# Product-key scatter: one 256-column matmul for each token, low halves added by VectorE, low splits of the stage made by GpSimd

## What is computed

```python
v_half, i_half = lax.top_k(s, PEER_TOPK)
...
experts = (i1 * PEER_KEYS + i2).reshape(T, PEER_HEADS * PEER_TOPK)
gates = jax.nn.softmax(best, axis=-1).reshape(T, PEER_HEADS * PEER_TOPK)
...
u = expert_u[eb]
act = jax.nn.gelu(jnp.einsum('td,tkd->tk', xb, u), approximate=False) * gb
return jnp.einsum('tk,tkd->td', act, expert_v[eb])
```

## Time and profile before

| | us |
|---|---|
| median of 3 runs (1753.81 to 1756.58) | 1756.58 |
| the profiled execution, time | 1751.53 |
| its span in the profile | 1749.9 |
| TensorE busy | 1689.0 (97%) |
| VectorE busy | 1303.8 (75%) |
| ScalarE busy | 1023.4 (58%) |
| GpSimd busy | 119.4 (7%) |

### The profile page before, as it was taken

How to read it: one execution, slowest core, us unless ns; L and a number is a source line. 1 busy time by engine, 2 the same in 40 slices (tenths; PEclk the granted TensorE clock), 3 DMA queues, 4 the chain that set the end, 5 groups by cost and what they waited for, 6 DMA issues and landing times.

```text
span 1749.9 us, 34534 instructions
## 1 busy us (share of the span) xinstructions
PE 1689.0 (97%) x10926; PEld 1521.9 (87%) x10926; DVE 1303.8 (75%) x2377; ACT 1023.4 (58%) x1567; POOL 119.4 (7%) x105
## 2 busy tenths in 40 slices
PE   7999999999999999999999999999999998899997
PEld 7998889999999999988888888898878887778886
DVE  6866665599977777777777777789777777877776
ACT  7653445666656666655545555664476666666665
POOL 0022300234320000000000000000000000000000
PEclk9999999999999999999999999999999999999999
DMA  6542246476775555567777777553356554246553
GB/s 203 166 147 73 85 157 208 154 226 202 221 233 176 178 170 177 176 209 242 240 267 245 242 241 241 178 169 106 109 160 198 183 190 151 85 137 210 182 192 108
DMA packets 114411, 316.65 MB, mean 181 GB/s; under 512 B 12752, under 2 KB 45904, under 8 KB 113840
## 3 DMA queue, kind: packets, MB, share of 16 engines
q1 hardware_dynamic: 113504, 311.88, 55.4%
q0 software_dynamic: 848, 4.00, 0.7%
HBM read 296.95 MB, written 18.87 MB: 180 GB/s over the span
## 4 chain that ended last, share of the span: by engine, by line
PE 83%; DVE 10%; ACT 3%; issue 2%; DMA 1%; POOL 1%; ACTq 0%; DVEq 0%; SPq 0%
PE bank L324 10%; PE bank L325 10%; PE bank L326 10%; PE bank L259 9%; PE bank L260 9%; PE bank L280 9%; PE bank L261 9%; PE bank L284 5%; PE bank L1327 3%; DVE wlo L243 2%; PE bank L1769 1%; PE bank L1034 1%; ACT whi L235 1%; POOL wlo L1626 1%; DVE arena L1493 1%
## 5 line engine op out<-in xcount | busy, mean ns | idle before, releaser
L243 DVE TENSOR_TENSOR wlo<-raw,whi 128x1024 fp32r<-128x1024 f32 x495 | 608.0, 1230 | 148.7 <-ACT whi L235 138.1
L235 ACT ACTIVATE whi<-raw 128x1024 fp32r<-128x1024 f32 x524 | 550.1, 1052 | 45.0 <-PE bank L318 34.4
L259 PE MATMUL bank<-x,whi 128*128 128x256 f32 (+1 forms) x1728 | 508.6, 294 | 8.9 <-DVE wlo L243 4.0
L261 PE MATMUL bank<-x,wlo 128*128 128x256 f32 (+1 forms) x1728 | 492.0, 285 | 0.0
L260 PE MATMUL bank<-x,whi 128*128 128x256 f32 (+1 forms) x1728 | 491.7, 285 | 0.0
L259 PEld LDWEIGHTS bank<-x,whi 128*128 128x128 f32 x1728 | 331.8, 192 | 15.2 <-issue 13.1
L260 PEld LDWEIGHTS bank<-x,whi 128*128 128x128 f32 x1728 | 332.5, 192 | 0.1
L261 PEld LDWEIGHTS bank<-x,wlo 128*128 128x128 f32 x1728 | 331.6, 192 | 0.0
L324 PE MATMUL bank<-whi,yhi 128*128 128x512 f32 x816 | 320.1, 392 | 8.9 <-DVE ylo L1596 3.1
L325 PE MATMUL bank<-wlo,yhi 128*128 128x512 f32 x816 | 318.6, 390 | 0.0
L326 PE MATMUL bank<-whi,ylo 128*128 128x512 f32 x816 | 318.1, 390 | 0.0
(11 more groups left out here) (313 smaller groups left out, 1753.9 us busy)
## 6 DMA issues: line engine op xcount, KB each, us to landing
raw<-in_stream SPq DMA_DIRECT2D x524, 512.0 KB, 3.5
act_spill<-h SPq DMA_DIRECT2D x128, 128.0 KB, 3.2
h<-act_spill SPq DMA_DIRECT2D x128, 128.0 KB, 3.3
h<-in_x SPq DMA_DIRECT2D x1, 1024.0 KB, 5.3
arena<-in_keys POOLq DMA_DIRECT2D x1, 1024.0 KB, 6.3
h_spill<-h SPq DMA_DIRECT2D x1, 1024.0 KB, 8.0
arena<-h_spill POOLq DMA_DIRECT2D x1, 1024.0 KB, 7.3
arena<-in_g_final POOLq DMA_DIRECT2D x1, 512.0 KB, 9.2
```

Source lines behind the costliest of these rows:

```text
L235: nc.scalar.activation(whi[:, q * 1024:(q + 1) * 1024], raw[:, q * 1024:(q + 1) * 1024], ACT.Copy).then_inc(hi_ready, 1)
L243: nc.vector.tensor_tensor(wlo[:, q * 1024:(q + 1) * 1024], raw[:, q * 1024:(q + 1) * 1024], whi[:, q * 1024:(q + 1) * 1024].bitcast(F32), ...
L259: nc.tensor.matmul(bank[b][:, 0:T], whi[:, w], xhi[:, x], start=k == 0, stop=False)
L261: last = nc.tensor.matmul(bank[b][:, 0:T], wlo[:, w], xhi[:, x], start=False, stop=k == KT - 1)
```

## The change

For each token the one-hot of i1 (now HOT1) goes without the gate. The gate goes with i2: HOT2 is a tile of 128 x 256, with the gate's high part at column i2 of its left half and the low part at column i2 of its right half. One fp32r matmul of 256 columns gives both halves of the token's part of G side by side in PSUM. ScalarE copies the high halves of four tokens to G (`g_high`), and VectorE adds the low halves to it in place (`sums`, with one input and the output in G, at the step of 256 words). The PSUM banks are declared as one tensor, and a slab's four tokens take two banks. `I1T` and `GT_COLS` now stay in PSUM; the gate's two parts (`GATES`), `I2T` and `iota` are in SBUF.

VectorE has four instructions for single tokens (`one_token`, a scalar_tensor_tensor over 256 elements), two for pairs of tokens (`two_tokens`, a tensor_tensor over 256) and a sum for each slab. It makes no low splits in this stage: GpSimd makes all 64 (`low_split`). TensorE takes a token behind every second chunk (k = 1, 3, 5, 7), and a slab's `slabs_done` comes ahead of its last token. Buffers: HOT1 holds four tokens, HOT2 two.

```diff
+        banks = ctx.enter_context(nc.psum_tensor("bank", [P, 8 * 512], F32))
+        bank = [banks[:, i * 512:(i + 1) * 512] for i in range(8)]
...
-                if between and k == KT // 2 - 1:
-                    between()
-            last.then_inc(slabs_done, 1)
+                if k == KT - 1:
+                    last.then_inc(slabs_done, 1)
+                if between:
+                    between(k)
...
+        GATES = h[:, 4 * SEQ:6 * SEQ].rearrange("p (s t) -> p s t", s=2)
+        I1T, I2T = bank[6][:, 0:SEQ], h[:, 6 * SEQ:7 * SEQ]
+        GT_COLS = bank[7][:, 0:SEQ]
...
+        HOT1 = (ylo[:, 0:SEQ], ylo[:, SEQ:2 * SEQ])
+        HOT2 = [yhi[:, b * SEQ:(b + 1) * SEQ].rearrange("p (s k) -> p s k", s=2) for b in range(2)]
+        SUMS = [banks[:, (2 + 2 * b) * 512:(4 + 2 * b) * 512].rearrange("p (t s k) -> p t s k", s=2, k=P)
+                for b in range(2)]
...
+            def token(i, r, y):
+
+                pe.wait_ge(s("hot_a"), i * (4 * TPS) + r * TPS + y + 1)
+                if y % 2 == 0:
+                    pe.wait_ge(s("hot_b"), i * 8 + r * 2 + y // 2 + 1)
+                if y == 0:
+                    pe.wait_ge(s("g_sum"), i * 4 + r + 1)
+                nc.tensor.matmul(SUMS[r % 2][:, y, :, :], HOT1[y // 2][:, y % 2 * P:(y % 2 + 1) * P], HOT2[y % 2],
+                                 start=True, stop=True).then_inc(s("hot_free"), 1)
...
-                up(pe, N_U + E1, U_U + E1, i, r, 4, SEQ, between=lambda: pair(i, r, 0))
-                pair(i, r, 1)
+                up(pe, N_U + E1, U_U + E1, i, r, 4, SEQ, between=lambda k: token(i, r, k // 2) if k % 2 else None)
...
-                nc.scalar.activation(dst, bank[2 + r % 2][:, 0:TPS * KEYS].rearrange("p (t k) -> p t k", k=KEYS),
-                                     ACT.Copy).then_inc(s("g_evac"), 1)
+                nc.scalar.activation(dst, SUMS[r % 2][:, :, 0, :], ACT.Copy).then_inc(s("g_high"), 1)
...
-                chain.link(nc.vector.tensor_copy(h[:, 4 * SEQ:6 * SEQ], bank[4][:, :]))
+                chain.link(nc.vector.tensor_copy(I2T, bank[6][:, SEQ:2 * SEQ]))
                 dve.wait_ge(s("gate_cols"), 1)
+                chain.link(nc.vector.tensor_tensor(GATES[:, 1, :], GT_COLS, GATES[:, 0, :], ALU.subtract))
...
+            def one_token(k0, i, r, y):
+                n = i * (4 * TPS) + (k0 + r) * TPS + y
                 dve.wait_ge(s("hot_free"), n - 2 + 1 + TPS)
+                own = slice(n, n + 1) if isinstance(n, int) else bass.ds(n, 1)
+                nc.vector.scalar_tensor_tensor(out=HOT2[y % 2], in0=iota[:, :].unsqueeze(1).to_broadcast([P, 2, P]),
+                                               scalar=I2T[:, own], in1=GATES[:, :, own].to_broadcast([P, 2, P]),
+                                               op0=ALU.is_equal, op1=ALU.mult).then_inc(s("hot_a"), 1)
+
+            def two_tokens(k0, i, r, z):
+                n = i * (4 * TPS) + (k0 + r) * TPS + 2 * z
+                dve.wait_ge(s("hot_free"), n - 4 + 2 + TPS)
+                c2 = I1T[:, n:n + 2] if isinstance(n, int) else I1T[:, bass.ds(n, 2)]
+                nc.vector.tensor_tensor(HOT1[z].rearrange("p (t k) -> p t k", k=P),
+                                        iota[:, :].unsqueeze(1).to_broadcast([P, 2, P]),
+                                        c2.unsqueeze(2).to_broadcast([P, 2, P]),
                                         ALU.is_equal).then_inc(s("hot_b"), 1)
 
+            def sums(k0, i, r):
...
+                dve.wait_ge(s("g_high"), k + 1)
...
+                nc.vector.tensor_tensor(dst, dst, SUMS[(k0 + r) % 2][:, :, 1, :], ALU.add).then_inc(s("g_sum"), 1)
+
+            def step(k0, i, r, first=False, last=False):
+                one_token(k0, i, r, 1)
+                two_tokens(k0, i, r, 1)
+                one_token(k0, i, r, 2)
+                one_token(k0, i, r, 3)
+                if not first:
+                    sums(k0 - 1, i, r)
+                if not last:
+                    two_tokens(k0 + 1, i, r, 0)
+                    one_token(k0 + 1, i, r, 0)
...
+            sums(KEYS - E1 - 1, 0, 0)
+            dve.wait_ge(lo_ready, N_V + AHEAD)
...
+            def low_split(i, r):
+                q = slot(N_U + E1 + AHEAD, r)
+                pool.wait_ge(lo_ready, at(N_U + E1 + AHEAD, i, r, 4))
+                pool.wait_ge(hi_ready, at(N_U + E1 + AHEAD, i, r, 4) + 1)
+                nc.gpsimd.tensor_tensor(wlo[:, q * 1024:(q + 1) * 1024], raw[:, q * 1024:(q + 1) * 1024],
+                                        whi[:, q * 1024:(q + 1) * 1024].bitcast(F32), ALU.subtract)\
+                    .then_inc(lo_ready, 1)
+
+            steps(pool, KEYS - E1, 4, low_split)
```

More of the change, by code:

```diff
@@ L151, in build @@
         arena = sb("arena", 32768)
-        bank = [ctx.enter_context(nc.psum_tensor(f"bank{i}", [P, 512], F32)) for i in range(8)]
+        banks = ctx.enter_context(nc.psum_tensor("bank", [P, 8 * 512], F32))
+        bank = [banks[:, i * 512:(i + 1) * 512] for i in range(8)]
         def V(name, i=0, n=1):
@@ L1310, in pe_peer @@
                                          GATE[:, tt * NHK:(tt + 1) * NHK])):
-                    last = nc.tensor.transpose(bank[4 + x // 2][:, (x % 2) * SEQ + tt * P:(x % 2) * SEQ + (tt + 1) * P],
+                    last = nc.tensor.transpose(bank[6 + x // 2][:, (x % 2) * SEQ + tt * P:(x % 2) * SEQ + (tt + 1) * P],
                                                src, ident[:, :])
@@ L1339, in act_peer @@
         def act_peer(act, chain):
-            act.sem_inc(s("g_evac"), 2)
+            act.sem_inc(s("g_sum"), 2)
             turn_act(act, T_WQ)
@@ L1378, in act_peer @@
             act.wait_ge(s("h_spilled"), 16)
-            nc.scalar.activation(GT_COLS, bank[5][:, 0:SEQ], ACT.Copy).then_inc(s("gate_cols"), 1)
+            nc.scalar.activation(GATES[:, 0, :].bitcast(F32R), GT_COLS, ACT.Copy).then_inc(s("gate_cols"), 1)
             for k in range(COLS_AT, E1):
@@ L1558, in four_tokens @@
[L1558 to L1563, removed]
-                                        ALU.is_equal).then_inc(s("hot_b"), 1)
@@ new lines, in sums @@
+            def sums(k0, i, r):
+                k = at(k0, i, r, 4)
+                dve.wait_ge(s("g_high"), k + 1)
+                g3 = G[:, :].rearrange("p (k t) -> p t k", t=SEQ)
+                dst = g3[:, k * TPS:k * TPS + TPS, :] if isinstance(k, int) else g3[:, bass.ds(k * TPS, TPS), :]
+                nc.vector.tensor_tensor(dst, dst, SUMS[(k0 + r) % 2][:, :, 1, :], ALU.add).then_inc(s("g_sum"), 1)
[9 more added lines that the diff above has]
+                    one_token(k0 + 1, i, r, 0)
@@ L1582, in prod @@
+            two_tokens(0, 0, 0, 0)
+            one_token(0, 0, 0, 0)
+            step(0, 0, 0, first=True)
+            steps(dve, KEYS - E1 - 2, 4, lambda i, r: step(1, i, r))
+            step(KEYS - E1 - 1, 0, 0, last=True)
+            sums(KEYS - E1 - 1, 0, 0)
+            dve.wait_ge(lo_ready, N_V + AHEAD)
             def prod(k0, i, r):
@@ L1598, in prod_lo @@
                     .then_inc(y_lo, 1)
-            dve.wait_ge(s("g_evac"), KEYS - E1 + 2)
+            dve.wait_ge(s("g_sum"), KEYS - E1 + 2)
             prod(0, 0, 0)
```

17 lines of the change are left out of this document (4 added, 13 removed).

## The result

The changed kernel takes 1865.57 us (median of 4 runs, 1863.56 to 1868.71), against 1756.57 for the kernel before: a ratio of 1.063, with a 95% interval of 1.0615 to 1.0643. That is 109 us more. The profiled execution took 1868.71 us, with a span of 1867.1. The two profiled executions lie 117 us apart, 8 more than the medians: the one of the kernel before took 1751.5, one of its shortest, and the one of the change was the longest of its four.

What follows compares the result with a forecast made beforehand. TensorE's own instructions were taken to bound the scatter stage; VectorE tokens held by GpSimd's splits would raise a slab from 3.76 to 5.30 us. 1751.5 + 98.6 (64 slabs) + 1.1 (last sum) = 1851 us, range 1785 to 1905.

Steps and rivals of the forecast that it cites:

- case one: Scatter slab: GpSimd's split holds token 2; its matmul and the last six chunk matmuls follow, 5.34 us a slab.
- the two heaps: Sign in the scatter's token instructions on VectorE: durations fall into two groups, 0.48 and about 2 us.
- the 0.28: Sign on VectorE in the scatter: held token instructions end 0.28 us after a GpSimd split.
- the 64 splits of 2.4: Sign on GpSimd in the scatter: 64 low splits of 2.4 to 2.8 us each.
- the loop: Scatter: slab's end, gelu, high split, GpSimd's split, held token, remaining matmuls, next slab's end; taken as 5.30 us a slab.
- the two cases: Scatter: token 2 held, 5.34 us each slab; or token 3, then next slab's token 0, 5.34 or 5.19 each.
- The preparation of the columns: Done once: a copy halved, a subtraction of 256 added; with the moved slab semaphore under 0.5 us, taken as nothing.
- (a): Rival, scatter: tokens are held but the phases fit, 4.28 us a slab, 1786 us in all; chance 0.09.
- (b): Rival, scatter: a sum of 1.55 us leaves VectorE never idle, 5.57 a slab, 1868, or 5.9 and 1890; chance 0.11.
- (c): Rival, scatter: TensorE's clock falls to 1.2 GHz after idling, 45 us on top of 1844: 1889 us; chance 0.15.
- (d): Rival, scatter: tokens aren't held; 1727 us at TensorE's 3.36 a slab, 1748 if a ring of 3.69 binds; chance 0.08.
- a ring: Scatter with free tokens: token 1's matmul, token 3, sum, one-hots, token 0, back to token 1's matmul: 3.69 us.

Runs made afterwards that it cites:

- the fastest version: The change with gates in PSUM, sum ahead of token 3, G's step only in the sum's write, and ScalarE's copy ahead of its high split: 1735.2 us.

## Why the prediction was right, and where not

**The mechanism and its price.** 1851 us was forecast and 1865.6 measured. The decisive step, that a token instruction with two SBUF inputs can't run beside GpSimd's split and ends 0.28 behind it, is shown twice: by the trace of the change (607.62 to 607.91) and by the gates in PSUM, which free the tokens and give back 86.6 us. There 127 token instructions run wholly inside a split of GpSimd, and none is held. Which token is held, the prediction left open; it is case one, token 2, in 63 of 64 slabs, at 5.33 of the 5.34 forecast.

**One reading was weaker than it was put.** That an operation with one input in PSUM isn't held was read from 0.27 "in the midst of GpSimd's". That row starts at 200.97, where GpSimd's ends at 201.13: the two overlap by 0.16 only, and the 0.27 is also the only price that was taken for such an instruction. The conclusion holds, by the 127 of the run with the gates in PSUM. Of the signs named, the two heaps, the 0.28 and the 64 splits of 2.4 came; TensorE idled for (240.00 - 173.45) / 44.1 = 1.5 us a slab (44.1 slabs of 5.44) where 1.9 was said, and the sum took 1.36 instead of 1.10.

**Terms of the loop.** Three were off and cancel, which is luck. The prediction had 0.12 + 0.72 = 0.84 from the held token's matmul to token 3's. It is 0.93, since the first matmul behind a wait takes 0.38 and the next starts 0.22 later. Against these 0.09, GpSimd starts 0.08 behind the high split instead of 0.15, and TensorE 0.12 behind VectorE instead of 0.14. The gelu's 0.20, the high split's 0.28 and 1.05, the split's 2.39 and the 0.28 behind it are as in the earlier trace rows.

**From 5.34 to 5.41.** Every fourth slab takes 5.66: the split's starts at 610.57 and 616.23, where 605.23 to 610.57 is 5.34. That is where the loop over four slabs turns, and ScalarE shows it:

```profile
614.60 0.38 ACT L1363 ACTIVATE h<-bank 128x256 f32<-128x256 f32 x1 [3.11 <-PE bank L262]
615.09 1.06 ACT L236 ACTIVATE whi<-raw 128x1024 fp32r<-128x1024 f32 x1
```

The gelu starts 0.30 behind token 3's matmul (614.30) instead of 0.20, and the high split 0.49 behind the gelu instead of 0.28. The slab behind it takes 5.42. It wasn't in the sum: the mean of the four is 5.44, and the first slab, 3.48 with nothing held yet, brings the stage's mean to 5.41. I had taken 5.30, between the two cases, so 0.11 a slab or 7 us in 64 were too little.

**The sum of the change.** Of the span's +117.2 (1867.1 - 1749.9), the stage is 344.9 - 239.1 = +105.8, where the prediction had +98.6. Behind the stage come +4.8 instead of +1.1. The last sum makes an idle stretch of TensorE of 4.14 us (2.63 in the earlier trace rows), +1.5; after it the matmuls start 0.43 apart and the stretch 873 to 886 has a clock of 0.74, where 757 to 770 had 1.00, another +2.6.

```profile
874.10 0.77 PE L326 MATMUL bank<-whi,yhi 128*128 128x512 f32 x1 [4.14 <-DVE ylo L1609]
874.67 0.63 PE L327 MATMUL bank<-wlo,yhi 128*128 128x512 f32 x1
875.09 0.63 PE L328 MATMUL bank<-whi,ylo 128*128 128x512 f32 x1
```

The prediction counted the sum's own time and not the clock behind it. The last 0.7 comes far behind, in code that both kernels share. The remaining +6.6 lies ahead of the scatter, in shared code too: in 120 to 140 us the clock was 0.83 instead of 1.00, and in 220 to 240 it was 0.74 instead of 0.92. Why, no run tells; it is most of the 8 us by which the profiled executions lie further apart than the medians. In the fastest version it was 0.91 and 0.83 there, and its stage begins 3.6 later than before's. The preparation of the columns costs nothing, as assumed: from TensorE's last wait ahead of it to the first scatter matmul are 28.2 us (496.57 to 524.8) against 28.8.

**The sum over G.** 1.10 was taken, 1.36 measured, inside the bounds of 0.685 and 1.55. In the change itself this makes no difference, since it lies in the shadow of the held token. It counts as soon as the tokens are free.

**The rivals.** (a), phases that fit at 4.28, didn't come: with two tiles of HOT2 nothing can be stored up. (b), a sum dear enough to keep VectorE busy, didn't either: its 1.36 lies below the 1.55. (c), the lower clock, came in the kernel without a step in G, where TensorE idles for 2.28; in the change its waits are 0.56 and 0.91 long, 1.24 where the loop turns, and the clock is 1.00. (d), tokens that aren't held, is the kernel with the gates in PSUM, at 1779 instead of 1748, for a ring that is 0.47 longer than forecast.

**What stands and what is open.** The cheaper matmul is real: TensorE alone has 3.36 a slab, and the last version comes within 0.07 of it. The low splits on GpSimd cost 44 to 47 us in the old kernel. In the new one the holding costs some 87 with the splits on GpSimd, and having them there instead of on VectorE, in this order of work, 17. With the gates in PSUM no wait for them shows. Taking the step out of the copy's write and the sum's read gave 29 us, and the order of copy and high split 19, once the tokens are free. Not settled is why the clock is at 0.95 in the change with the sum ahead of token 3, and at 1.00 in the change: TensorE's idle stretches are much alike (0.46 and 1.05, and at most 1.27, against 0.56, 0.91 and at most 1.24). Nor is it known whether the fastest version owes something to GpSimd at all: it wasn't tried with the splits on VectorE. The 3.3 us that VectorE has to do for each slab there, with 1.15 more for a split, are more than the 3.43 of a slab, which speaks against it, but that is argued and not shown.

## What to carry to other kernels

Before work goes from VectorE to GpSimd, list the operands of what stays on VectorE in those stretches. In these traces an instruction with one of its tensors in PSUM runs on. One with two tensors in SBUF, or a tensor_scalar from SBUF to SBUF, stands still for as long as a single GpSimd instruction lasts, and so does what is queued behind it. Operands in SBUF alone don't decide: in the kernel before, the search for the top 16, on one tensor in SBUF, goes on inside GpSimd's split of 365.48 to 367.89 in its usual time.

```profile
365.51 0.41 DVE L1441 MAX8 arena<-arena 128x8 f32<-128x256 f32 x1
```

A move of an operand, or shorter GpSimd instructions, can be worth more than the work that was moved. And when a held engine is freed, walk the ring through the smallest buffer at once, with each wait's order on every engine in it: here it took three more steps, of 4, -29 and -19 us, before the cheaper matmul was worth anything.

## What was not expected of the hardware

- A step of 256 words in G costs each side of VectorE's 512-element sum: 0.68 us with none, 1.09 where only the write has it, 1.36 where read and write have it. ScalarE's copy of 512 takes 0.59 dense and 1.10 with it. The Trainium skill ("VectorE: DVE Perf Modes", the section on the TRN2 errata) gives one formula for an fp32 tensor_tensor, an estimate of 0.69 for 512 elements; the dense run agrees, and the other two don't.
- What holds VectorE is a single instruction of GpSimd: with four GpSimd instructions of 0.85 in the mean instead of one of 2.39, a token's mean time fell from 920 ns to 538.
- A tensor_scalar over 128 elements with a single tensor input in SBUF and two column operands is held too, 1.88 for two instead of 0.60. How far behind GpSimd's end a held instruction ends goes with its form: 0.08 for this one, 0.28 for the token's 256 elements, and 0.41 for a tensor_tensor over 384 in the kernel before (163.92 + 1.21 = 165.13, beside a GpSimd instruction that ends at 164.72).
- TensorE's first matmul behind a wait takes 0.38 instead of 0.28, and the next one starts 0.22 behind it instead of 0.12.
- After 2.28 us idle (G without a step) and after 4.14 (the transition of the change) TensorE's clock was at the lower level; after 2.63 in the kernel before it stayed at the full one. The length of the pause alone doesn't decide.
- A loop written out for four slabs costs at its turn: 5.66 instead of 5.34 in the change, where ScalarE comes late, and some 3.66 instead of 3.36 in the fastest version, where TensorE is the one that binds.
